# Adding a result block to the residual stream before, not after, the low parts of the previous block's transposes

## The reference, cut to what matters

```python
q = (xn @ x_wq[l]).reshape(b, s, X_HEADS, X_HEAD_DIM)
...
h = h + o @ x_wo[l]                                  # (512 x 512) @ (512 x 2048)

xn = rms_norm(h, norm_mlp[l])
h = h + jnp.square(jax.nn.relu(xn @ mlp_w1[l])) @ mlp_w2[l]
```

## Time and profile before

| what | value |
|---|---|
| median of three runs | 2830.89 us |
| profiled execution, its own time | 2830.58 us |
| profiled execution, span from first to last instruction | 2828.9 us |
| TensorE busy | 2756.9 us, 97% of the span |
| VectorE busy | 1195.1 us, 42% |
| ScalarE busy | 825.2 us, 29% |
| mean granted TensorE clock | 0.996 |
| the product with x_wo | about 1344.1 to 1394.3 us of the span |

### The profile page before, as it was taken

The page is one execution under the profiler, slowest core; times in us unless marked ns, Lnnn a source line. Parts: engine busy times, 40 slices in busy tenths (PEclk is TensorE's granted clock), DMA queues, the critical chain, the costliest instruction groups (busy, mean ns, idle before and its releaser), DMA issues.

```text
span 2828.9 us, 44631 instructions
## 1 busy us (share of the span) xinstructions
PE 2756.9 (97%) x18532; PEld 2177.3 (77%) x18532; DVE 1195.1 (42%) x1838; ACT 825.2 (29%) x1358; POOL 123.3 (4%) x238
## 2 busy tenths in 40 slices
PE   7999999999999999998999999999999999999997
PEld 6777777777767766786888888888888888888885
DVE  3245556566533554444524333233332333323333
ACT  3222222222223544344422221222212222122222
POOL 3000010111112011000000000000000000000000
PEclk9999999999999999999999999999999999999998
DMA  3321111111125432221232322223223232232322
GB/s 129 107 80 48 47 47 46 52 47 49 59 79 188 163 99 69 75 90 53 82 97 90 101 93 96 96 90 101 91 95 96 91 101 91 95 96 92 100 92 109
DMA packets 71470, 249.25 MB, mean 88 GB/s; under 512 B 8784, under 2 KB 8912, under 8 KB 69408
## 3 DMA queue, kind: packets, MB, share of 16 engines
q1 hardware_dynamic: 64512, 222.59, 24.4%
q0 software_dynamic: 6816, 24.60, 2.6%
HBM read 236.93 MB, written 10.22 MB: 87 GB/s over the span
## 4 chain that ended last, share of the span: by engine, by line
PE 93%; DVE 3%; ACT 1%; issue 1%; DMA 1%; DVEq 0%; POOL 0%; SPq 0%; ACTq 0%
PE ps L1075 27%; PE ps L1076 26%; PE ps L1077 25%; PE ps L1102 8%; PE ps L1310 1%; PE ps L1289 1%; PE ps L1081 1%; PE ps L1298 1%; PE ps L1096 0%; DVE w_lo L695 0%; ACT pad L416 0%; ACT w_hi L416 0%; DMA h<-in_mem 0%; DMA x_mix<-in_x 0%; PE ps L1161 0%
## 5 line engine op out<-in xcount | busy, mean ns | idle before, releaser
L695 DVE TENSOR_TENSOR w_lo<-w_raw,w_hi 128x1024 fp32r<-128x1024 f32 (+2 forms) x440 | 505.2, 1149 | 1232.0 <-ACT w_hi L416 1231.7
L416 ACT ACTIVATE w_hi<-w_raw 128x1024 fp32r<-128x1024 f32 (+2 forms) x440 | 439.1, 999 | 1523.6 <-PE ps L1077 1523.3
L1075 PE MATMUL ps<-act_hi,w_hi 128*128 128x512 f32 x1792 | 731.3, 408 | 7.0 <-ACT pad L416 4.7
L1077 PE MATMUL ps<-act_hi,w_lo 128*128 128x512 f32 x1792 | 700.6, 391 | 0.0
L1076 PE MATMUL ps<-act_lo,w_hi 128*128 128x512 f32 x1792 | 699.7, 390 | 0.0
L1076 PE MATMUL ps<-w_lo,mid_hi 128*128 128x512 f32 x1088 | 433.9, 399 | 0.0
L1075 PE MATMUL ps<-w_hi,mid_hi 128*128 128x512 f32 x1088 | 429.8, 395 | 1.4 <-DVE mid_lo L1021 1.4
L1077 PE MATMUL ps<-w_hi,mid_lo 128*128 128x512 f32 x1088 | 426.7, 392 | 0.0
L1075 PEld LDWEIGHTS ps<-act_hi,w_hi 128*128 128x128 f32 x1792 | 336.4, 188 | 101.3 <-issue 18.0
L1077 PEld LDWEIGHTS ps<-act_hi,w_lo 128*128 128x128 f32 x1792 | 336.7, 188 | 72.5
L1076 PEld LDWEIGHTS ps<-act_lo,w_hi 128*128 128x128 f32 x1792 | 337.0, 188 | 68.4 <-issue 5.8
(11 more groups left out here) (268 smaller groups left out, 2443.7 us busy)
## 6 DMA issues: line engine op xcount, KB each, us to landing
w_raw<-in_w_rest SPq DMA_DIRECT2D x320, 512.0 KB, 3.6
w_raw<-in_w_pairs SPq DMA_DIRECT2D x112, 384.0 KB, 3.1
x_mix<-in_x SPq DMA_DIRECT2D x4, 1024.0 KB, 8.1
qk<-scr_qkv POOLq DMA_DIRECT2D x16, 256.0 KB, 3.9
h<-in_x POOLq DMA_DIRECT2D x4, 1024.0 KB, 11.9
out<-h SPq DMA_DIRECT2D x4, 1024.0 KB, 4.3
scr_qkv<-pad POOLq DMA_DIRECT2D x15, 256.0 KB, 2.8
w_raw<-in_w_lora SPq DMA_DIRECT2D x8, 288.0 KB, 7.4
```

Source lines behind the costliest of these rows:

```text
L416: return nc.scalar.activation(dst, src, ACT.Copy, scale=scale)
L695: V.tensor_tensor(dst, w_raw[:, slot, 0:dst.shape[-1]], high.bitcast(F32), ALU.subtract).then_inc(s["w_split"], 1)
L1075: mm(dst, a_hi, b_hi, start=start, stop=False)
L1077: return mm(dst, a_lo, b_hi, start=False, stop=stop)
```

## The change

In VectorE's program for the product with x_wo, the call of `add_set` is put ahead of the call of `turned_lo`. It acts at u = 3, 5 and 7, where both calls are made; at u = 1 there is only `add_set`. No instruction is added or removed, and no other engine's program changes.

```diff
             for u in range(UNITS):
                 lo_next(G_XO, u)
+                if u % 2:
+                    add_set(UNITS * G_XO + u + 1, (S_XO + u // 2) % 2, u // 2)
                 if u % 2 and u > 1:
                     turned_lo(3, u // 2 - 1, 3, tiles_of(act_hi), tiles_of(act_lo))
-                if u % 2:
-                    add_set(UNITS * G_XO + u + 1, (S_XO + u // 2) % 2, u // 2)
```

## The result

| kernel | median of 5 runs, us | lowest to highest |
|---|---|---|
| before | 2830.62 | 2828.45 to 2830.95 |
| changed | 2845.89 | 2844.33 to 2847.59 |

The ratio is 1.0055, with a 95% interval of 1.004 to 1.0069. The forecast was slower, 2841.4 us, range 2840.2 to 2844.8. The direction is right; the size isn't, and the range was missed at its upper end. The profiled execution took 2847.2 us with a span of 2845.5, which is 16.6 us over the span of before.

A forecast was written before the change was run, and what follows sets the result against it. TensorE, without slack behind the change, was taken to bound the kernel. Three places at 3.56 us, 10.7 us in all, on the profiled 2830.58 gave 2841.3, stated as 2841.4 us with the median's offset; range 2840.2 to 2844.8.

The forecast's parts named there:

- What bounds the kernel, and no slack behind the change: TensorE, busy 97% of the span, has no wait from 1382 to 2809 us, so each microsecond lost moves the end.
- Nothing removed: At the ends of units 3, 5 and 7 the adds wait for TensorE and can't start earlier; gain zero.
- 3.56 us per place, 10.7 in all: Ends of units 3, 5, 7: next unit starts 3.49 us later, plus 0.07 for the restart; three places 10.7 us.
- T + 3.72: Predicted start of unit 4, counted from the start T of unit 3's last matmul; before, T + 0.23.
- The weights' low part is covered: On VectorE behind the adds, unit 5's weights' low part moves back 2.6 us but stays covered, 2.7 us to spare.
- The clock, "I add nothing for it and hold it as a rival": At the three 3.33 us pauses TensorE returns before the clock would fall; nothing added to the sum.
- Rival 1: Clock falls at one or more of the three pauses, up to 1.7 us each: 2843.1, 2844.8 or 2846.5; chance 0.19.
- never for the short ones: Claim that the trace before shows the clock falling once, for one long wait, and not for short waits.
- rival 2: Order makes no difference: act_lo tiles or their banks needed over 3.5 us after unit 4's start; 2830.9 us, chance 0.03.
- rival 3: Faster: adds at the three places come forward by up to 2.6 us each, at most to 2823.0 us; chance 0.01.

The follow-up runs named there:

- the kernel with the filler: Changed kernel plus nine useless matmuls on TensorE in each of the three pauses, 27 in all; 2841.66 us against 2845.65 for the changed kernel run again.
- adds2: Changed kernel with two adds ahead of the four act_lo tiles and two behind, at units 3, 5 and 7; 2840.26 us (before 2830.31).
- adds3: Changed kernel with three adds ahead of the four act_lo tiles and one behind, at units 3, 5 and 7; 2842.23 us (before 2830.31).
- split_pause: Changed kernel with VectorE doing two adds, one act_lo tile, two adds, three tiles at units 3, 5 and 7; 2843.54 us (before 2830.31).
- lala: Changed kernel with VectorE alternating act_lo tile and add, tile first, at units 3, 5 and 7; 2838.85 us (before 2830.44).

## Why the prediction was right in direction and wrong in size

- **What bounds the kernel, and no slack behind the change**: right. TensorE has no wait after 1411 us, and the whole difference lies in the stretch.
- **Nothing removed**: right. The adds still start 0.43 us after the last matmul (1368.05 to 1368.48).
- **3.56 us per place, 10.7 in all**: right. T + 3.72 came to the hundredth, and the kernel with the filler measures 10.7 us.
- **The weights' low part is covered**: right. There is no wait on `w_lo`, and with it at the same lateness the filler run loses nothing to it.
- **The clock, "I add nothing for it and hold it as a rival"**: this step failed. The clock fell at all three places in both profiled executions of the changed kernel, at 1.5 us each, and 3.0 where the half clock lasted 6.8 us. Rival 1 with three falls, priced at 2846.5, is what happened (2845.9), and it had 0.19 as a whole. The Trainium skill (TensorE: Matmul & The Clock Gate, section "HAM oscillation — how this bites in real kernels") warns of this kind of loss, a clock that falls back in the waits between bursts and costs again at each. The eight waits of 3.3 us in four traces agree with it; the waits of 1.6 us and less here kept the clock. The warning pointed to rival 1, and the prediction gave that 0.19 all the same.

How the step went wrong can be read in the kernel before. I looked at its longest wait, 4.2 us, and at the many short ones of cross-attention, up to 1.6 us, and placed 3.3 us between them. I reasoned that the fall had come over 4 us after the last matmul and that TensorE would be back before that, as if the clock fell at once or not at all. In the changed kernel it fell 1.3 us after TensorE was back (1371.77 to about 1373.1). And I left out a row. These are the wait of TensorE and the windows around it in the trace of before:

```profile
178.52 1.73 PE L1102 MATMUL ps<-eye,v_s 64*64 64x64 f32 x32 [2.26 <-DVE v_s L781]
```

```profile
178.00:179.00 1.00, 0.48 (x14) 0.52 (x16) 1.00 (x3) 0.60 (x1) 0.00 (x0) 0.92 0.00 0
179.00:182.00 3.00, 3.00 (x27) 2.55 (x25) 2.06 (x3) 1.46 (x3) 0.00 (x0) 0.50 0.05 9
```

A wait of only 2.26 us, and the clock at 0.50 behind it. So it was wrong that the trace shows the fall "never for the short ones". One more wait between matmuls is over 2 us in the kernel before, and that one kept the clock:

```profile
36.03 0.47 PE L1075 MATMUL ps<-act_hi,w_hi 128*128 128x512 f32 x1 [2.32 <-DVE w_lo L695]
```

```profile
36.00:40.00 4.00, 3.97 (x17) 3.31 (x18) 1.22 (x2) 0.15 (x1) 3.41 (x11) 1.00 0.68 210
```

Whoever had asked the windows for every wait over 2 us between matmuls, not for the longest alone, would have found two of three that lost the clock, one of them shorter than 3.3 us, and reason to put falls into the sum: two make about 2844.5, three about 2846 (2841.3 and 1.5 to 1.7 for each).

The price of a fall was also a little off: 1.7 us by the clock's mean, 1.5 measured ((1480.8 - 1476.4) / 3), since the distance between matmuls of 512 columns goes from 0.233 to 0.427 us, less than double. On the rivals that lost: the order did matter (rival 2), and nothing came forward (rival 3).

What stays open is what decides whether a pause of 2.1 or 2.7 us loses the clock. Alike pauses of one execution differed in it, and so did one and the same wait in different executions: that of 2.26 us at 178 us lost the clock in 7 of 14 traces, that of 2.32 us at 36 us in 3 of 14.

## What to carry to other kernels

Where TensorE has no slack, putting work that it waits for behind work that waits for it costs the whole length of both, and it can be summed from durations and answer times to a tenth of a microsecond. Then ask what the pause does to the clock: look up the granted clock behind every wait of the kernel at hand, not just behind the longest, and price the fall where a pause is as long as those that lost it here: surely at 3.3 us, and with a chance, not as a certainty, from 2.1 to 2.7 us. If a pause can't be avoided, cut it into short ones or give TensorE idle work: 27 useless matmuls gained 4 us here.

## What the runs showed of the hardware that was not expected

- Pauses of 0.94 and 1.53 us (three each) left the granted clock at 1.00. Of those of 2.13 us two in three lost it in adds2, of those of 2.73 us two in three in adds3, and both of 2.7 us near 907 us kept it. All eight of 3.3 us lost it (three and three in two traces of the changed kernel, one each with one place alone), and so did all twelve of 4.1 to 4.2 us near 905 us.
- Two in three overstates the short ones. Over the 14 traces there are 34 waits of 2.1 to 2.3 us (with the kernel's own at 36 and 178 us, and those of split_pause), and 14 of them lost the clock.
- Four pauses of 0.9 and 0.3 us within 4.7 us, with three matmuls between them, kept it, at all three places of lala.
- The clock can fall after TensorE has resumed, 1.3 us after in the first pause shown. The half clock then lasted 3.4 us; in two traces it lasted 6.8 us at one place.
